# Ten expert passes in mixed order, and three quarters of a projection moved behind them

## What is computed

```python
x = x + gt1 * x_mix
x = x + gt2 * hier_moe(modulate(rms_norm(x, norm2_g[l]), sh2, sc2), *moe_args)
...
return rms_norm(x, final_norm_g)
...
hx = rmsnorm(x, g_pre[l]) * (1 + scale[:, None]) + shift[:, None]
hc = rmsnorm(ctx, g_pre[l]) * (1 + scale_c) + shift_c
if l % 2 == 0:
    yx, yc = mlstm_pool_mixer(hx, hc, ab_w_in[j], ..., not last)
...
x = x + gate[:, None] * rmsnorm(yx, g_post[l])
if not last:
    ctx = ctx + gate_c * rmsnorm(yc, g_post[l])
```

## Time and profile before

| | |
|---|---|
| time before, median of 3 runs | 1808.34 us (1799.67 to 1808.34) |
| the profiled execution's own time | 1805.27 us |
| its span, first to last instruction | 1803.5 us |
| PE busy | 1586.6 us (88%) |
| DVE, ACT busy | 488.0 us, 339.2 us |
| mean granted TensorE clock | 0.922 of full speed |
| DMA | 397.57 MB, 220 GB/s over the span |
| experts' passes, first weight load to last down step | 566.8 to 1184.6 us |

### The profile page before, as it was taken

The page is one execution under the profiler, slowest core; times in us unless marked ns, Lnnn a source line. Parts: engine busy times, 40 slices in busy tenths (PEclk is TensorE's granted clock), DMA queues, the critical chain, the costliest instruction groups (busy, mean ns, idle before and its releaser), DMA issues.

```text
span 1803.5 us, 21928 instructions
## 1 busy us (share of the span) xinstructions
PE 1586.6 (88%) x9261; PEld 1078.5 (60%) x9261; DVE 488.0 (27%) x1222; ACT 339.2 (19%) x698; POOL 4.1 (0%) x8
## 2 busy tenths in 40 slices
PE   5799949898988878997998999976889999979797
PEld 2555649777877334453455664455676685867566
DVE  2200164541224241122213100024343231020581
ACT  2211230112121111202110001023112122121371
POOL 0000000000000000000000000000000000000000
PEclk9999966799978989998999999986899999989999
DMA  9577750132224989999999999951313313322000
GB/s 346 218 297 280 297 245 1 47 123 113 94 96 170 421 333 370 399 398 419 403 409 410 411 419 405 384 210 36 140 47 140 135 52 140 144 100 103 38 1 24
DMA packets 54304, 397.57 MB, mean 220 GB/s; under 512 B 6360, under 2 KB 13689, under 8 KB 16441
## 3 DMA queue, kind: packets, MB, share of 16 engines
q1 hardware_dynamic: 40384, 341.85, 47.4%
q10 hardware_dynamic: 13240, 52.16, 7.3%
q0 software_dynamic: 576, 2.10, 0.3%
HBM read 389.80 MB, written 6.29 MB: 220 GB/s over the span
## 4 chain that ended last, share of the span: by engine, by line
PE 76%; DMA 8%; DVE 8%; ACT 4%; issue 2%; PEld 1%; SPq 0%; ACTq 0%; PEldq 0%; DVEq 0%
PE bank L660 14%; PE bank L1373 12%; PE bank L1388 8%; PE bank L2300 6%; DMA work<-in_moe_w_up 4%; PE bank L2317 4%; PE bank L1488 3%; PE bank L1493 3%; PE bank L518 2%; PE bank L2286 2%; PE bank L689 2%; PE bank L1095 2%; PE bank L1083 2%; PE bank L840 1%; DMA work<-in_ab_pool_w 1%
## 5 line engine op out<-in xcount | busy, mean ns | idle before, releaser
L660 PE MATMUL bank<-H,ring 128*128 128x256 f32 (+1 forms) x928 | 244.4, 424 | 18.2 <-DVEq L294 8.2
L660 PEld LDWEIGHTS bank<-H,ring 128*128 128x128 f32 x928 | 178.8, 194 | 78.4 <-issue 49.3
L2300 PE MATMUL bank<-ring,work 128*32 128x512 f32 (+1 forms) x768 | 142.8, 656 | 19.2 <-DMA work<-in_moe_w_up 10.4
L1373 PE MATMUL bank<-H,work 128*128 128x256 f32 x512 | 116.7, 387 | 0.3 <-issue 0.3
L1373 PE MATMUL bank<-H,ring 128*128 128x256 f32 x512 | 112.9, 381 | 0.0
L1373 PEld LDWEIGHTS bank<-H,work 128*128 128x128 f32 x512 | 97.7, 193 | 19.6 <-issue 6.4
L1373 PEld LDWEIGHTS bank<-H,ring 128*128 128x128 f32 x512 | 98.1, 192 | 13.6
L2300 PEld LDWEIGHTS bank<-ring,work 128*32 128x32 f32 (+1 forms) x768 | 37.2, 126 | 111.9 <-issue 87.8
L1388 PE MATMUL bank<-work,H 128*128 128x512 f32 x192 | 85.2, 597 | 0.0
L1388 PE MATMUL bank<-ring,H 128*128 128x512 f32 x192 | 83.0, 592 | 0.0
L2317 PE MATMUL bank<-ring,work 128*32 128x512 f32 (+1 forms) x384 | 66.9, 611 | 2.8 <-issue 2.2
(11 more groups left out here) (403 smaller groups left out, 2010.5 us busy)
## 6 DMA issues: line engine op xcount, KB each, us to landing
ring<-in_moe_w_gate SPq DMA_DIRECT2D x48, 1024.0 KB, 11.6
ring<-in_moe_w_up SPq DMA_DIRECT2D x48, 1024.0 KB, 9.6
ring<-in_moe_w_down SPq DMA_DIRECT2D x48, 1024.0 KB, 12.1
work<-in_ab_w_in ACTq DMA_DIRECT2D x28, 1024.0 KB, 10.2
ring<-in_ab_w_in SPq DMA_DIRECT2D x14, 2048.0 KB, 7.5
ring<-in_ada_w SPq DMA_DIRECT2D x12, 2048.0 KB, 7.6
ring<-in_w_in SPq DMA_DIRECT2D x12, 2048.0 KB, 7.5
ring<-in_w_mod SPq DMA_DIRECT2D x12, 2048.0 KB, 7.7
```

The source lines that it names most:

```text
L660: mm = nc.tensor.matmul(bank[i % NB][:, 0:n], weight(c, k, j * P, (j + 1) * P), rhs(k), start=(k == 0), stop=(k == kt - 1))
L1373: mm = nc.tensor.matmul(b[:, j * T:(j + 1) * T], w_k(m, n, k, at, at + P), H[:, k, m.s], start=(k == 0), stop=(k == DT - 1), skip_group_ch ...
L2300: mm = nc.tensor.matmul(bank[b][rows, :], gath[:, k, rows], half_slot[(load_at[n + half] + e) % NHALF][:, (k % 4) * 512:(k % 4 + 1) * 512] ...
```

## The change

The passes are put in the order two, four, four, two, four, two, four, four, two, four experts. `FILL_FOUR` goes from 16 steps to 13, `FILL_TWO` from 2 to 3, `start` from 4 to 6. The body ends after the first of the four OUT chunks (`OUT_EARLY`). The other three (`OUT_LATE`) run in `last1_*`, woven with the first block's last norm; that norm and the second block's first are computed from two sums of squares at once, so H is made directly from X. The context's two norms (`post`, `after`) run inside `mix_*`. SP waits for the stored rows before it loads the weights of the next stage.

```diff
+PASSES = [(2 * i, 2) for i in range(N_WIDE // 2)] + [(N_WIDE + 4 * i, 4) for i in range((NX - N_WIDE) // 4)]
+PASSES = [PASSES[i] for i in (0, 4, 5, 1, 6, 2, 7, 8, 3, 9)]
+NPASS = len(PASSES)
...
-        NORM_BANK = (7, 6, 1, None, None, 0, None, None, None, 7)
+        NORM_BANK = (7, 6, 1, 0, 1, None, None, None, None, 7)
...
-                    self.yo = flat_tiles(self.pp, DT, T)
+                    self.yo = work[:, WORK - DT * T:WORK].rearrange("p (n t) -> p n t", t=T)
...
-                nc.scalar.activation(H[:, 2 * r:2 * r + 2, m.s], halves, ACT.Square).then_inc(sq_ready, 2)
+                if m.hf == 1:
+                    nc.scalar.activation(H[:, 2 * r:2 * r + 2, m.s], halves, ACT.Square).then_inc(sq_ready, 2)
...
+            if m.hf == 0:
+                for k in range(DT):
+                    nc.scalar.activation(H[:, k, m.s], m.yo[:, k, :], ACT.Square).then_inc(sq_ready, 1)
...
+        OUT_EARLY, OUT_LATE = (0,), (1, 2, 3)
...
-        FILL_FOUR, FILL_TWO = (2, 2, 2, 2, 2, 2, 2, 1, 1), (0, 0, 0, 1, 0, 1, 0, 0, 0)
+        FILL_FOUR, FILL_TWO = (2, 1, 1, 1, 2, 2, 1, 2, 1), (0, 0, 1, 1, 0, 0, 0, 1, 0)
...
-            for _ in range(4):
+            for _ in range(6):
...
-                if p == NPASS - 1:
-                    nc.vector.sem_inc(moe_ring_free, 1)
-                else:
+                if p < NPASS - 1:
...
-                    nc.vector.sem_inc(moe_ring_free, 1)
+                    nc.vector.sem_inc(moe_ring_free, 2)
...
-            yield from out_pe(pe, m)
-            yield from norm_steps_pe(pe, m)
-            yield from norm_steps_pe(pe, m)
+            yield from out_pe(pe, m, OUT_EARLY)
...
-            yield from out_act(act, m)
-            yield from post_act(act, m)
-            yield from next_act(act, m, x_new, 0, mod2, 24)
+            yield from out_act(act, m, OUT_EARLY)
...
+            out = out_pe(pe, mixers[0], OUT_LATE)
             for j in range(DT):
                 if j >= 4:
                     pe.wait_ge(accT_out, j - 3)
                 for t in range(TT):
                     mm = nc.tensor.transpose(bank[j % 4][:, t * P:(t + 1) * P], acc[:, t, j * P:(j + 1) * P], ident[:])
                 mm.then_inc(accT_mm, 1)
-            norm_pe(pe, H, T)
+            take(out, 2)
+            u = norm_use["pe"]
+            pe.wait_ge(accT_out, DT)
+            for i, src in enumerate((sq_x, sq_g)):
+                for k in range(DT):
+                    pe.wait_ge(sq_ready, DT * (u + i) + k + 1)
+                    for j in range(4):
+                        mm = nc.tensor.matmul(bank[i][32 * j:32 * j + 32, 0:64], ones[:, 0:32], src[:, k, j * 64:(j + 1) * 64],
+                                              start=(k == 0), stop=(k == DT - 1), skip_group_check=True)
+                mm.then_inc(sumsq_done, 1)
+            take(out, 2)
+            norm_use["pe"] += 2
+            for i in range(2):
+                pe.wait_ge(rinv_done, u + i + 1)
+                for j in range(4):
+                    mm = nc.tensor.matmul(bank[2 + i][:, j * 64:(j + 1) * 64], bc(ident[:, 32 * j:32 * j + 1], [P, P]), rstd[:, (u + i) % 2, 0:64],
+                                          start=True, stop=True, skip_group_check=True)
+                mm.then_inc(rstd_mm, 1)
+            finish(out)
...
-            act.wait_ge(accT_out, DT)
-            squares_act(act, X, H, slice(0, T))
-            std_act(act, T)
+            m = mixers[0]
+            out = out_act(act, m, OUT_LATE)
+            for k in range(DT):
+                act.wait_ge(accT_out, k + 1)
+                nc.scalar.activation(sq_x[:, k, :], X[:, k, 0:T], ACT.Square).then_inc(sq_ready, 1)
+            for k in range(DT):
+                nc.scalar.activation(sq_g[:, k, :], X[:, k, 0:T], ACT.Square, scale=vec("fng", k, k + 1)).then_inc(sq_ready, 1)
+            u = norm_use["act"]
+            norm_use["act"] += 2
+            act.wait_ge(sumsq_done, STD_BEFORE[u])
+            nc.scalar.activation(rstd[:, u % 2, 0:64], bank[0][:, 0:64], ACT.Sqrt, bias=epsc[:], scale=1.0 / D).then_inc(std_done, 1)
+            take(out, 4)
+            act.wait_ge(fused, 1)
+            nc.scalar.activation(rstd[:, (u + 1) % 2, 0:64], rstd[:, (u + 1) % 2, 0:64], ACT.Sqrt, bias=epsc[:]).then_inc(std_done, 1)
+            finish(out)
+            modulate_act(act, mod2, 0, (0,))
...
+            L, V = chain.link, nc.vector
+            coef_dve(chain, vec("gpre", 0, 8), mod2, 8, (0,))
+            L(V.tensor_tensor(coef[:, 0, :], coef[:, 0, :], vec("fng"), ALU.mult))
...
+                V.scalar_tensor_tensor(out=X[:, j, 0:T], in0=bank[j % 4][:, 0:T], scalar=mod1[:, 40 + j, 0:1],
+                                       in1=X[:, j, 0:T], op0=ALU.mult, op1=ALU.add).then_inc(accT_out, 1)
+            u = norm_use["dve"]
+            norm_use["dve"] += 2
+            r, g = rstd[:, u % 2, 0:64], rstd[:, (u + 1) % 2, 0:64]
+            dve.wait_ge(std_done, STD_BEFORE[u])
+            V.reciprocal(r, r).then_inc(rinv_done, 1)
+            dve.wait_ge(rinv_done, u + 1)
+            dve.wait_ge(sumsq_done, STD_BEFORE[u + 1])
+            L(V.scalar_tensor_tensor(out=g, in0=bank[1][:, 0:64], scalar=1.0 / D, in1=r, op0=ALU.mult, op1=ALU.mult))
+            V.tensor_tensor(g, g, r, ALU.mult).then_inc(fused, 1)
+            dve.wait_ge(std_done, STD_BEFORE[u + 1])
+            L(V.reciprocal(g, g))
+            V.tensor_tensor(g, g, r, ALU.mult).then_inc(rinv_done, 1)
+            finish(out_dve(dve, mixers[0], OUT_LATE))
+            dve.wait_ge(a_mm, turns["dve_a"])
+            dve.wait_ge(rstd_mm, STD_BEFORE[u + 1])
             for k in range(DT):
-                nc.vector.scalar_tensor_tensor(out=X[:, k, 0:T], in0=X[:, k, 0:T], scalar=vec("fng", k, k + 1), in1=rows[:, 0:T],
-                                               op0=ALU.mult, op1=ALU.mult).then_inc(x_first, 1)
+                mod_use["dve"] += 1
+                V.scalar_tensor_tensor(out=H[:, k, 0:T], in0=X[:, k, 0:T], scalar=coef[:, 0, k:k + 1], in1=bank[3][:, 0:T],
+                                       op0=ALU.mult, op1=ALU.mult).then_inc(scaled, 1)
+            for k in range(DT):
+                V.scalar_tensor_tensor(out=X[:, k, 0:T], in0=X[:, k, 0:T], scalar=vec("fng", k, k + 1), in1=bank[2][:, 0:T], op0=ALU.mult, op1=ALU.mult)
...
-            finish(norm_steps_pe(pe, m))
+            post = norm_steps_pe(pe, mixers[0])
+            after = norm_steps_pe(pe, mixers[0])
             gates_pe(pe, m)
             finish(tiles_pe(pe, m, Q[0]))
             finish(tiles_pe(pe, m, K[0]))
             finish(rows_pe(pe, m, V[0]))
             finish(gate_cols_pe(pe, m))
             finish(weave(both(mlstm_pe(pe, m, 0), mlstm_pe(pe, m, 1)), both(tiles_pe(pe, m, PU[0], False), tiles_pe(pe, m, PU[1], False)), 3, 1))
+            next(post)
             finish(rows_pe(pe, m, O[0]))
+            finish(post)
             finish(rows_pe(pe, m, Z[0]))
             finish(pool_pe(pe, m))
             finish(heads_pe(pe, m, 0))
             finish(tiles_pe(pe, m, Q[1]))
+            next(after)
             finish(tiles_pe(pe, m, K[1]))
+            finish(after)
...
+            next(post)
             finish(o_act(act, m, 0))
+            finish(post)
             finish(z_act(act, m, 0))
             finish(tiles_act(act, m, Q[1], raw_act))
+            next(after)
             finish(tiles_act(act, m, K[1], raw_act))
+            finish(after)
...
+            next(post)
             finish(o_dve(dve, m, 0))
+            finish(post)
             finish(z_dve(dve, chain, m, 0))
             finish(mixed_dve(dve, m))
             finish(heads_dve(dve, m, 0))
-            for c in range(4):
-                conv_dve(dve, chain, m, 4 + c)
+            for c in (4, 5):
+                conv_dve(dve, chain, m, c)
+            next(after)
+            for c in (6, 7):
+                conv_dve(dve, chain, m, c)
+            finish(after)
...
+            for i in range(2):
+                sp.wait_ge(rows_stored[i], 16 * (NPASS // 2))
             for j in range(len(second)):
                 load_chunk(sp, AT_SECOND + j)
```

More of the change, by code:

```diff
@@ L1904, in pg_dve, with out_dve @@
                 yield
-        def out_dve(dve, m):
-            for r in range(4):
+        def out_dve(dve, m, rs=range(4)):
+            for r in rs:
                 yield
```

40 lines of the change are left out of this document (18 added, 22 removed).

## The result

The changed kernel takes 1838.24 us (median of 4 runs, 1833.22 to 1842.14), the kernel before 1806.57 us beside it (1799.67 to 1808.34). The ratio is 1.0178, 95% interval 1.0146 to 1.0210: slower by 1.8%, where 1812 us and a range of 1795 to 1829 were forecast.

What follows compares the result with a forecast made beforehand. Expert-weight transfers were taken to set the stage's pace, with PE's body work hidden in them. Stage -41.0, behind it +37.7 and mixer +10.0 sum to +6.7 us on 1805.3: 1812 us, range 1795 to 1829.

Steps and rivals of the forecast that it cites:

- So PE should hold the transfers up nowhere for long: Experts' stage: with 13 tile steps a pass over four takes PE 72.0 us against 79.3 of transfers, so transfers seldom wait.
- The longest PE stretch with no slot released: Passes over four, last projection step to first down step: falls from 22.1 to 18.6 us, under 20.5 of weight transfer.
- four steps of buffer: Passes over two experts: have four steps of weight buffer and now stand between the dense passes over four.
- 3 at the start, 9 at the end: Experts' stage: the only two losses left in the changed kernel, 3 us at its start and 9 at its end.
- the 30 of the prediction: Kernel before, experts' stage: 617.8 us against 588 for 241.1 MB at 410 GB/s, so 30 us lost.
- its loss of 15.7 us in 640 to 814: Kernel before, experts' stage: 15.7 us lost at 373 instead of 410 GB/s, put down to the two-step buffer.
- 32 to 37: Sign in the changed profile: passes over two take 32 to 37 us, those over four 62 to 80.
- The rest of the stage: Experts' stage of the changed kernel: 232.7 MB moved at 412 GB/s, 564.8 us.
- Behind the stage: Last down step to the gates' end: 104.1 us for 66.4, 37.7 more, from moved body and OUT work and waits.
- a sign of error: Behind the stage: the prediction is wrong if gathered rows land later than 30 us behind the last down step.
- In the mixer: Context norms: two times 5 us of squares, sums and spread added, 10 us; bounds 5 and 18.
- Slower, the stage keeps its gaps: Rival, chance 0.35: PE still holds slots in tile-dense passes over four, 15.7 us return, stage ends at 1159, time 1828.

Runs made afterwards that it cites:

- after_half_pe: The changed kernel with the body's tiles and rows multiplied over every second k tile only, loads and waits kept: 1802.65 us (one run), stage 570.4 us.
- fused_only: The kernel before with only the two norms behind the experts made one: 1803.44 us, ratio to before 1.0007.
- after_mended: The changed kernel with body steps moved to each pass's early experts, context norms' squares earlier, and SP's next-stage loads held until the gathered rows landed: 1822.44 us.
- load_after_rows: The changed kernel with the old order of passes, and SP's next-stage loads held until the gathered rows have landed: 1835.12 us, ratio to before 1.0158.
- rest_only: The changed kernel with the old order of passes (six over four, then four over two): 1844.96 us, ratio to before 1.0253.

## Why the prediction was wrong

**The step that failed** is "So PE should hold the transfers up nowhere for long", and under it "The longest PE stretch with no slot released ... 18.6, under the 20.5 us which two steps of weights take". The stretch itself was right: in the pass over four that ends at 1046 SP issues four loads from 1019.86 on and the next at 1038.08, 18.2 us later. What it was held against was wrong. Two steps of weights are pending only when nothing has landed since they were released. When the transfers have caught up, only the last release is pending: 10.2 us of transfer in a pass over four. In that stretch the DMA engines run out of work at about 1031, 11 us after the release, and the share falls to 0.49:

```profile
1030.00:1037.00 7.00, 7.00 (x39) 2.50 (x41) 1.06 (x3) 2.31 (x4) 0.00 (x0) 1.00 0.49 167
```

In the pass over two shown above at most 10.2 us were pending against 12.1, where I had counted on four steps of buffer. after_half_pe shows the size: 29.1 us for PE's hold, of which my sum held 12 (3 at the start, 9 at the end). The stage was forecast at 576.8 us and took 599.5: 22.7 too long, 20 of them losses of this kind and the rest bytes. Of the whole loss 12 us lie in the first 80 us of the stage, where the sum had 3: SP has nothing to issue until 593.16, and again from 624.6 to 637.63. after_half_pe moves 413 and 410 GB/s there.

The gaps didn't shrink, they grew: against its bytes at 412 GB/s the kernel before loses 617.8 - 245.9 / 0.412 = 21 us, the changed one 599.5 - 233.8 / 0.412 = 32. (The window of before holds 617.8 x 398 = 245.9 MB, 4.8 more than I had counted, so its loss was smaller to begin with than the 30 of the prediction. Most of that are two loads of 2 MB for the next stage, which SP issues at 1169.04 and 1169.43; in the changed kernel they wait for the stored rows.)

A second premise failed for the kernel before. The prediction puts its loss of 15.7 us in 640 to 814 down to tile steps that fill PE, and says of the mLSTM steps that PE has far less to do in them. The largest gap there, 6 us at 642 to 650, is in an mLSTM step that waits for VectorE; fewer tile steps in a pass take nothing from it.

From end to end of the last copy of rows, the passes over two took 40.3 to 47.1 us where I had 32 to 37, those over four 57.0 to 77.1; the first figure is no proof of a gap, since it is 40.5 to 45.7 in after_half_pe too: the large sets of the next pass are loaded in it.

**The rest of the stage was right:** the bytes (232.7 MB forecast, 599.5 us x 390 GB/s = 233.8) and the rate: with PE's hold gone they come at 412 GB/s, the rate I took. The page "DMA: Bandwidth & Descriptors" of the Trainium skill, section Bandwidth, has beside its 358 GB/s a transfer of 16 MB at 425 GB/s with the core alone on its memory; the trace lies near the second figure.

**Behind the stage** 104.1 were forecast and 106.2 measured. The terms are off both ways. The largest excesses are PE's idle time ahead of the transposes (8.9 us for 1.5 + 5.2) and the first OUT chunk, which ran at a granted clock of 0.89 (15.8 for 14.2); PE's wait with the two spreads was shorter than put (3.7 for 5.5). That the rows land 34.0 us behind the last down step (1193.33 - 1159.3) was named as a sign of error; it cost only 0.41 us, as the body steps cover it.

**In the mixer** +10 was forecast, +13.4 measured. Sums, spreads and the two waits make 2 x 2.37 + 2 x 1.00 + 0.96 + 1.08 = 8.8. The remaining 4.6 is in PE's busy time, which rises by 14.3 us (512.87 for 498.58) where the sums and spreads are 6.7, at a granted clock of 0.94 for 0.96. fused_only has 7.1 us of the same kind, in a mixer that it doesn't edit, at the same 0.94. Why the low stretches fall differently there is open, and with it how much of the 13.4 the norms cost.

**The rival "Slower, the stage keeps its gaps"** is what happened, at 1828 us. Of the gaps of the kernel before, it returned 15.7; 22.7 came. That and the 3.4 of the mixer and 2.1 behind the stage make 28.2 us over the forecast, less 7.0 from the stretch ahead of the stage: 21, which is what 1831.3 is over the 1810.2 of the table. That its stage end, 1159, is the measured one to 0.3 us is luck: the stretch ahead was 7.0 us shorter. The mechanism of the case, slots held by PE, is what was found; its place, the dense passes over four, holds for two of the gaps, while others are at the start and in the last pass over two. Its chance, 0.35, was too low.

## What to carry to other kernels

Work that hides under transfers is free only while loads are pending for as long as that work lasts: compare each stretch of the computing engine between two releases with the bytes that are still pending when it begins, which can be those of the last release alone, not with the size of the whole buffer. Look for waits inside the hidden work too: a wait for a third engine holds a slot as long as arithmetic does. Before moving hidden work out, halve its arithmetic and keep its loads: the fall of the stage (10 us here before the change, 29 after it) says how much of the loss is that work's. And compare what PE's busy time does with what each stretch does. Taking 46.5 us of PE's work and 12 MB out of the stage gave back 18.3 us; behind the stage PE's busy time rose by 45.7 us (86.65 for 40.93) and the stretch by 39.7, in the mixer by 14.3 and 13.4.

## What the runs showed of the hardware

The time of a gather depended on what else was in flight. The same four indirect gathers of GpSimd (0.5 MB each) took 4.5 to 5.3 us to land in after_mended, 8.1 to 9.1 in load_after_rows, 11.4 to 23.9 in the changed kernel, and 15.0 to 29.1 in rest_only. In the last two SP issued three loads of 2 MB within 1 us of the first of them, in load_after_rows only ScalarE's two loads of 1 MB stood ahead of them, and in after_mended nothing did. By a page of the Trainium skill ("DMA: Bandwidth & Descriptors", Queues, rings and completion order) each DMA engine takes packets from its queues in turn; that would share the engines between the loads and the gathers. The traces agree with it so far as the order of landing goes: in rest_only gathers land at 1188.9, 1197.3 and 1203.5, and loads that were issued ahead of the second gather at 1184.6, 1193.2, 1194.5 and 1201.8.
